# Attention scores of a two-layer encoder: first head's products, then the second's, in place of alternating between them

## The reference

```python
# layer 0, mixer A: 8 query heads, 2 key heads, 128-frame window, bias, sink
scores = jnp.einsum('bcqkgd,bcskd->bckgqs', qc, kb).astype(jnp.float32) * HEAD_DIM ** -0.5
# layer 0, mixer B: 8 heads, strictly causal, stick-breaking
z = jnp.einsum('bhqd,bhsd->bhqs', qb, kh) * scale
# layer 1, mixer C: 16 heads, own chunk of 64 frames and 8 before it
sc = jnp.einsum('bqhd,bshd->bhqs', qc, kc).astype(jnp.float32) * scale + bias
```

## Time and profile before

| | us |
|---|---|
| median of 3 runs | 2770.37 |
| lowest and highest run | 2765.73 and 2771.34 |
| profiled execution, its own time | 2767.64 |
| span of the profiled execution | 2765.9 |

### The profile page before, as it was taken

The page is one execution under the profiler, slowest core; times in us unless marked ns, Lnnn a source line. Parts: engine busy times, 40 slices in busy tenths (PEclk is TensorE's granted clock), DMA queues, the critical chain, the costliest instruction groups (busy, mean ns, idle before and its releaser), DMA issues. The chain is left out here.

```text
span 2765.9 us, 35451 instructions
## 1 busy us (share of the span) xinstructions
PE 2304.8 (83%) x12564; PEld 1860.9 (67%) x12564; DVE 1811.8 (66%) x2399; ACT 1423.3 (51%) x1705; POOL 584.0 (21%) x448
## 2 busy tenths in 40 slices
PE   6299998892999999995299999988929999999960
PEld 5176776781788888884277777766827888888840
DVE  2165445536888888984835444455367888998848
ACT  2145344311777777773334444444116777777732
POOL 0000224112222333320600000001122223322306
PEclk8699999995999999997599999999959999999985
DMA  7610101323899999995411111103237999999953
GB/s 142 87 39 16 31 16 31 125 76 133 311 369 366 370 373 371 374 373 230 154 33 33 33 50 41 33 32 110 85 136 282 376 382 382 377 363 357 361 220 153
DMA packets 128187, 541.33 MB, mean 196 GB/s; under 512 B 35904, under 2 KB 76880, under 8 KB 101456
## 3 DMA queue, kind: packets, MB, share of 16 engines
q1 hardware_dynamic: 108320, 504.73, 50.2%
q0 software_dynamic: 18432, 33.60, 3.2%
q10 hardware_dynamic: 1328, 1.59, 0.5%
HBM read 515.21 MB, written 58.20 MB: 207 GB/s over the span
## 5 line engine op out<-in xcount | busy, mean ns | idle before, releaser
L324 DVE TENSOR_TENSOR arena<-arena,arena 128x2048 fp32r<-128x2048 f32 (+1 forms) x454 | 943.5, 2112 | 160.8 <-ACT arena L663 78.4
L1579 ACT CAST arena<-arena 128x2048 fp32r<-128x2048 f32 x380 | 705.0, 1918 | 179.7 <-PE psum L1373 107.5
L1373 PE MATMUL psum<-arena,arena 128*128 128x512 f32 x3072 | 737.2, 396 | 8.1 <-DVE arena L324 8.1
L1373 PEld LDWEIGHTS psum<-arena,arena 128*128 128x128 f32 x3072 | 571.3, 189 | 124.5 <-issue 5.7
L555 PE MATMUL psum<-arena,arena 128*128 128x512 f32 x2016 | 510.9, 405 | 22.8 <-ACT arena L663 20.6
L555 PEld LDWEIGHTS psum<-arena,arena 128*128 128x128 f32 x2016 | 375.3, 192 | 119.1 <-ACT arena L663 21.2
L1384 PE MATMUL psum<-arena,arena 128*128 128x512 f32 x1536 | 367.9, 395 | 8.9 <-DVE arena L324 8.8
L1384 PEld LDWEIGHTS psum<-arena,arena 128*128 128x128 f32 x1536 | 288.6, 190 | 83.2 <-DVE arena L324 23.1
L324 DVE TENSOR_TENSOR arena<-psum,arena 128x512 fp32r<-128x512 f32 (+1 forms) x186 | 160.9, 872 | 223.6 <-ACT arena L675 118.4
L315 PE MATMUL psum<-ident,arena 128*128 128x128 f32 x1024 | 160.2, 300 | 145.1 <-POOL arena L915 73.4
L315 PEld LDWEIGHTS psum<-ident,arena 128*128 128x128 f32 x1024 | 147.4, 198 | 172.1 <-POOL arena L915 83.0
(11 more groups left out here) (143 smaller groups left out, 1951.5 us busy)
## 6 DMA issues: line engine op xcount, KB each, us to landing
arena<-in_moe_w_gate SPq DMA_DIRECT2D x64, 2048.0 KB, 10.7
arena<-in_moe_w_up SPq DMA_DIRECT2D x64, 2048.0 KB
arena<-in_moe_w_down SPq DMA_DIRECT2D x64, 2048.0 KB, 8.7
arena<-expert_rows SPq DMA_DIRECT2D x16, 1024.0 KB, 13.9
x_rows<-arena SPq DMA_DIRECT2D x24, 512.0 KB, 2.6
arena<-x_rows SPq DMA_DIRECT2D x24, 512.0 KB, 6.6
arena<-in_c_w_in SPq DMA_DIRECT2D x24, 512.0 KB, 4.3
arena<-in_x SPq DMA_DIRECT2D x16, 512.0 KB, 7.4
```

What stands on the lines that cost most here:

```text
L324: return eng.tensor_tensor(tile, src, high.bitcast(F32), ALU.subtract)
L1373: mm = pe.matmul(bank(o), cs[:, c * P:(c + 1) * P], ws[:, c * FF:(c + 1) * FF], start=(k == 0 and c == 0), stop=(k == 2 and c == CH - 1))
L1579: act.copy(w_hi[w][:, cols], self.raw[w][:, cols]).then_inc(hi_ready[w], 1)
```

## The change

The loop over heads moves from the innermost place to the outermost. The products, their operands, their banks and their waits stay.

```diff
-                    for a, w in places[0][1]:
-                        for k, (qs, ks) in enumerate(((q_hi, k_hi), (q_lo, k_hi), (q_hi, k_lo))):
-                            for h in range(2):
-                                own = slice(DH * h, DH * (h + 1))
-                                at = places[h][0] + a
+                    for h in range(2):
+                        own = slice(DH * h, DH * (h + 1))
+                        for a, w in places[h][1]:
+                            at = places[h][0] + a
+                            for k, (qs, ks) in enumerate(((q_hi, k_hi), (q_lo, k_hi), (q_hi, k_lo))):
                                 done[h] = pe.matmul(psum[:, at:at + w], qs[b][own, t * P:(t + 1) * P],
                                                     ks[kv][own, k0 + a:k0 + a + w], start=(k == 0), stop=(k == 2))
```

## The result

The changed kernel takes 2787.31 us (median of 5 runs, 2782.27 to 2792.28) against 2768.01 us before (5 runs, 2764.80 to 2771.34). The ratio is 1.0071, with a 95% interval of 1.0051 to 1.0090: slower by 19.3 us, where 53 were forecast. The profiled execution took 2787.31 us with a span of 2785.5, 19.7 more than the one before.

A forecast was written before the change was run, and what follows sets the result against it. TensorE's stream was taken to bound the attention stages. 51.4 us paid in full, minus 2.1 absorbed, plus 4 in steps without projections made 53 on 2767.6, 2821; predicted 2822, range 2812 to 2842.

The forecast's parts named there:

- The bound: Both attention stages: TensorE's own stream sets them, busy for 406.21 of 435 and 475.75 of 510 us.
- The worth of a pair: Score products: one of each head together cost about one product's time, 0.149 us at 320 columns.
- 2m - 1 pitches: Score group, m products per head: heads overlap only at the change-over, adding m - 1 product-start intervals; 62.2 us in all.
- m = 3: Score groups up to 512 keys, three products per head: two more start intervals each; 3.5, 9.8, 4.2 and 5.6 us.
- m = 6: Score groups over 512 keys, six products per head: five more start intervals each; 26.8, 3.5, 4.1 and 4.7 us.
- the wait on the projection's bank: Ten 512-column groups: the projection's load already waits for VectorE's copy, absorbing 0.21 us each, minus 2.1 us.
- steps without projections: Attention steps where TensorE's waits before transposes hide most of 10.8 us; 4 us taken as cost, bounds 0 and 10.8.
- VectorE's first read of a group: Head 0's scores end when they did before, so the VectorE and ScalarE chain starts as before; no gain.
- Rival 1: Score groups: heads don't meet even at the change-over; one start interval per group, 19.4 us, time 2841; chance 0.09.
- Rival 2: Score products: weight loads in the same half don't hide, about 0.11 us each, 88 us more, 2910; chance 0.04.
- Rival 3: Transposes: head 0's results come 0.745 us sooner, TensorE's waits vanish, faster, at most down to 2754; chance 0.02.
- Rival 4: Score products: heads never ran at once, trace starts only bookkeeping, nothing changes, time 2770; chance 0.02.

The follow-up runs named there:

- the last experiment: Kernel before, with products of probabilities and values of step s - 1 moved between the two parts of step s's transposes: 2732.98 us against 2767.61, ratio 0.9877.
- the kernel without overlap: Changed order plus a TensorE wait for head 0's finished scores before head 1's first product, against the kernel before: 2867.60 us against 2767.34, ratio 1.0361.

## Why the prediction was wrong

**The bound.** Right: TensorE's stream sets both attention stages, and what it pays is paid in the total. The exchange in the last experiment shows it, and so do the 100 us of the kernel without overlap.

**The worth of a pair.** Right: two products of different halves cost one product's time, at the pitches worked out, 0.149 at 320 columns. The group of 2.27 us with the wait between the heads fits them.

**The step that failed.** "Only the last of head 0 and the first of head 1 can still run together, so 2m - 1 pitches take the place of m: m - 1 more." It took program order for the order of starts. The runs put in its place: nothing up to m = 4, and m - 4 pitches and 0.10 us of start-up above. Term by term:
- m = 3, forecast 23.1 us: the groups last as before within 0.01 us each, so under 1 us.
- m = 6, forecast 39.1: 36 groups of 320 columns at 0.40 are 14.4, four of 512 at 0.55 are 2.2, and the eight between, at about 0.5, 4: 20.6 in all.

Forty of these 48 groups have projections behind them; they make 17 of the 20.6 us. The starts in the two profiles show them paid in full. From layer 1's first group of twelve that has projections behind it to the first group of its last pair, first before the change and then after:

```profile
1442.09 1.15 PE L574 MATMUL psum<-arena,arena 64*128 64x320 f32 x12
...
1840.14 0.55 PE L574 MATMUL psum<-arena,arena 64*128 64x128 f32 x6
```

```profile
1445.01 1.55 PE L574 MATMUL psum<-arena,arena 64*128 64x320 f32 x12
...
1854.63 0.56 PE L574 MATMUL psum<-arena,arena 64*128 64x128 f32 x6
```

That is 398.05 and 409.62 us, 11.6 more for 28 groups of twelve, 0.41 each. The first three "b" pairs, from their first group of twelve on, take 160.03 us before (from 281.94) and 166.04 after (from 278.98), 6.0 more for their 12 groups. So 17.6 of the 19.3 us are found group by group. The remaining 1.7 are less than what the interval (14 to 25 us) leaves open.

A hint was in the earlier trace rows: four loads were under way when only two products had begun. The prediction read it as a load pulled ahead of a product and did not ask whether products can be pulled ahead in the same way; it had a rival with less overlap than forecast and none with more.

**What is hidden.** The 2.1 us taken off for the wait on the projection's bank is without object, since the groups it belongs to did not get longer (1.11 us, still with the wait). Of the 4 us for steps without projections the totals say nothing, as the granted clock there differs between the two executions (0.94 from 1840.14 to 1868.07 before, 0.99 in the same steps, 1854.63 to 1881.75, after). But single groups show the hiding. These are a group of the last pair of layer 1 and its transposes before (the second row is the one in the earlier trace rows at 1861.84) and after, all at a clock of 1.00:

```profile
1860.12 1.14 PE L574 MATMUL psum<-arena,arena 64*128 64x320 f32 x12
```

```profile
1874.60 1.52 PE L574 MATMUL psum<-arena,arena 64*128 64x320 f32 x12
1876.32 1.12 PE L586 MATMUL psum<-ident,arena 128*128 128x128 f32 x8 [0.20 <-DVE arena L794]
```

Both times the transposes begin 1.72 us after the group. TensorE's wait for VectorE's scaling shrank from 0.57 to 0.20 us and took up the longer group.

**The other signs.** The step of 7.18 us was to become 7.92 and is 7.38 (1642.95 to 1650.33), and the score products' busy time was to rise to 175 us and is 138.9: both err by the same step as the total. TensorE's share stayed above 95%, as said: in the windows 300 to 360 and 1600 to 1700 of the earlier trace rows it is now 57.98 of 60 and 95.55 of 100 us.

**The other engines.** VectorE's first read of a group comes 1.18 us after the group's start before the change (1642.84 after 1641.66) and after it, as said. These are the rows of the changed kernel:

```profile
1650.33 1.55 PE L574 MATMUL psum<-arena,arena 64*128 64x320 f32 x12
...
1651.51 0.82 DVE L777 CUSTOM_DVE_ANT_0 arena<-psum,arena 128x640 f32<-128x640 f32 x1 [0.37 <-PE psum L574]
```

**The rivals.** Rival 1 (no overlap at the change of heads) would show 1.98 us for a group; it is 1.48. Rival 2 (loads exposed) would show 2.9; even without any overlap of heads the group is 2.27. The statement of the Trainium skill that goes with it ("TensorE: Matmul & The Clock Gate", Part 3, "What overlaps and what doesn't") is not borne out by that. The one beside it says that MATMULs start and end in strict program order. The trace disagrees: head 1's products start ahead of up to three of head 0's. Rival 3 (waits vanish) failed as argued: the wait of 0.24 us is still there at 1648.56. Rival 4 (the heads were never run at once) would have cost the kernel with the wait no more than its change-overs, 37 us at most; it cost 100.

## What to carry to other kernels

Products that use different halves of TensorE's array run together even when they don't alternate strictly: runs of up to four products per half cost nothing here. At 320 columns the fifth costs 0.25 us and the sixth 0.15 more. So count the run as the trace counts it, since one product of the program may be two records, and break longer runs. Where TensorE waits between two dependent parts of its own order, look for independent products further down in its stream: one exchange was worth 34.6 us, more than the whole change of order cost.

## What the runs showed of the hardware

- TensorE starts a product of a free half ahead of up to three unstarted ones of the busy half, for 64-row halves (runs of 3, 4, 5, 6) and for 64-column halves (runs of 6 to 16 records). Whether it counts products, or products with their loads, these runs don't tell, as every product has its own load. Nor do they tell one window over both halves from a short queue for each half.
- The products of probabilities and values stand twice in the trace (x20 for ten), the scores and the transposes once.
- A wait of TensorE for its own finished product, between two heads of six products of 320 columns, makes the group 0.29 us longer than twelve pitches and the fixed part (2.27 instead of 1.98 us).
